# Decode step: sample index and state outputs moved among the state tiles, value projection and gated unit into the top-k, sample state onto GpSimd

## The reference

```python
u, q, k, v, qi, ki, wi = split(rmsnorm(x) @ w_in)        # q, k: per-head norm and rotary; qi, ki: rotary
# state-space heads: 32 groups, 64 complex states each
bu = einsum('blgc,gpc->blgp', u, b_bar)
a_cum, h = associative_scan(combine, (lam_bar, bu)); h = h + a_cum * h0
y = real(einsum('blgp,gcp->blgc', h, c_mat)) + d_skip * u
y = gelu(y); y = y * sigmoid(y @ w_glu)
# sparse attention: 8 heads of 64
s = sum_h wi[h] * relu(qi[h] . ki)                       # the samples also score 256 cached keys each
idx = top_k(s, 64); attend over the chosen k, v
x = x + concat(y, attention) @ w_out
```

## Time and profile before

| | |
|---|---|
| median of 3 runs | 1687.07 us (1686.31 to 1692.87) |
| the profiled execution | 1684.85 us, its span 1683.0 us |
| TensorE, VectorE, ScalarE, GpSimd busy | 93%, 76%, 57%, 5% of the span |
| mean granted TensorE clock | 0.956 |
| loads at the start | params 1152 and 142 KB, x 1120 KB, consts 861 KB, weights of u 2048 KB |
| other transfers at the start | old pool history 448 KB, weights of qi 2048 KB, of kw 288 KB |

### The profile page before, as it was taken

The page is one execution under the profiler, slowest core; times in us unless marked ns, Lnnn a source line. Parts: engine busy times, 40 slices in busy tenths (PEclk is TensorE's granted clock), DMA queues, the critical chain, the costliest instruction groups (busy, mean ns, idle before and its releaser), DMA issues.

```text
span 1683.0 us, 23394 instructions
## 1 busy us (share of the span) xinstructions
PE 1571.4 (93%) x7789; PEld 1268.0 (75%) x7789; DVE 1274.4 (76%) x1704; ACT 963.7 (57%) x1222; POOL 87.2 (5%) x118
## 2 busy tenths in 40 slices
PE   5997949889999778999999999999999999999998
PEld 4653436479999666888888888888888888888887
DVE  8888561135554467988988998998998998988986
ACT  2110324134443226777777777777777777777774
POOL 0386100000000000000000000000000000000000
PEclk9998778999999977999999999999999999999999
DMA  5421012424535515998998998998998998998992
GB/s 217 150 76 50 30 54 72 140 100 161 190 120 172 203 35 187 356 378 305 353 374 310 347 373 312 348 370 312 355 358 324 349 363 320 348 362 325 348 358 94
DMA packets 212886, 420.79 MB, mean 250 GB/s; under 512 B 10233, under 2 KB 56469, under 8 KB 212572
## 3 DMA queue, kind: packets, MB, share of 16 engines
q1 hardware_dynamic: 211542, 414.37, 68.6%
q10 hardware_dynamic: 622, 3.45, 0.5%
q0 software_dynamic: 672, 2.32, 0.4%
HBM read 417.50 MB, written 3.07 MB: 250 GB/s over the span
## 4 chain that ended last, share of the span: by engine, by line
PE 83%; DVE 3%; issue 2%; ACT 1%; DMA 1%; SPq 0%; DVEq 0%; ACTq 0%
PE bank L1149 19%; PE bank L1154 19%; PE bank L1153 19%; PE bank L1027 3%; PE bank L1030 3%; PE bank L1031 3%; PE bank L1104 3%; PE bank L1010 2%; PE bank L1174 1%; PE bank L1112 1%; PE bank L1042 1%; PE bank L1046 1%; PE bank L1045 1%; PE bank L744 1%; DVE hT L1561 1%
## 5 line engine op out<-in xcount | busy, mean ns | idle before, releaser
L2047 DVE TENSOR_TENSOR split<-raw_w,split 128x1024 fp32r<-128x1024 f32 x672 | 783.3, 1220 | 50.6 <-ACT split L1498 48.5
L1498 ACT ACTIVATE split<-raw_w 128x1024 fp32r<-128x1024 f32 x672 | 684.4, 1060 | 109.3 <-PE bank L1149 108.1
L1149 PE MATMUL bank<-split,xgr 128*128 128x512 f32 x896 | 359.2, 401 | 3.7 <-DVE split L2047 3.7
L1154 PE MATMUL bank<-split,xgr 128*128 128x512 f32 x896 | 354.4, 396 | 0.0
L1153 PE MATMUL bank<-split,xgr 128*128 128x512 f32 x896 | 354.4, 396 | 0.0
L1149 PEld LDWEIGHTS bank<-split,xgr 128*128 128x128 f32 x896 | 169.3, 189 | 41.9 <-DVE split L2047 4.5
L1154 PEld LDWEIGHTS bank<-split,xgr 128*128 128x128 f32 x896 | 169.2, 189 | 39.9
L1153 PEld LDWEIGHTS bank<-split,xgr 128*128 128x128 f32 x896 | 169.4, 189 | 37.5
L1149 PE MATMUL bank<-split,hbr 128*128 128x512 f32 x448 | 177.9, 397 | 0.0
L1154 PE MATMUL bank<-split,hbr 128*128 128x512 f32 x448 | 176.9, 395 | 0.0
L1153 PE MATMUL bank<-split,hbr 128*128 128x512 f32 x448 | 176.9, 395 | 0.0
(11 more groups left out here) (377 smaller groups left out, 1913.6 us busy)
## 6 DMA issues: line engine op xcount, KB each, us to landing
raw_w<-in_moe_gate SPq DMA_DIRECT2D x112, 1024.0 KB, 5.4
raw_w<-in_moe_up SPq DMA_DIRECT2D x112, 1024.0 KB, 6.0
raw_w<-in_moe_down SPq DMA_DIRECT2D x112, 1024.0 KB, 5.2
ring<-in_w_gate SPq DMA_DIRECT2D x11, 1024.0 KB, 5.0
ring<-in_w_up SPq DMA_DIRECT2D x11, 1024.0 KB, 7.3
ring<-in_w_down SPq DMA_DIRECT2D x8, 1408.0 KB, 6.2
ring<-in_w_in SPq DMA_DIRECT2D x5, 2048.0 KB, 9.7
ring<-in_w_out SPq DMA_DIRECT2D x2, 2048.0 KB, 7.6
```

The source lines that it names most:

```text
L1149: first = mm(out, hi, place[:, s, 0, cols], start=start, stop=False)
L1154: last = mm(out, hi, place[:, s, 1, cols], start=False, stop=stop)
L1498: A(place[:, s, 0, :], raw_w[:, at:at + BLOCK], ACT.Copy).then_inc(sem("high_ready"), 1)
L2047: TT(place[:, s, 1, :], raw_w[:, at:at + BLOCK], place[:, s, 0, :].bitcast(F32), ALU.subtract).then_inc(sem("low_ready"), 1)
```

## The change

- **Order of fills.** The value projection leaves the state tiles; its three fills go before `glu`, behind it, and between the logits of t = 0 and t = 1. The sample index (`skT`, `wbd`) and the state outputs y 0 to 2 go among the state tiles, y 3 between the index dots of t = 0 and t = 1, `kt` behind the logits of t = 2.
- **State outputs.** The samples' y no longer needs the finished sample state: it is summed from `raw` through the same matrices as the prompt and from `hs0` = rates times h0, so two more 8-column matmuls per tile.
- **GpSimd** computes `hs0` before tile 0, the sample state and the last state behind tile 15, and fills `qbd`.
- **VectorE** does the factors and `norm` ahead of all doublings (`NORM_AT` = 1), the index queries behind the rotary of qi, the skip terms where y stands, the gelu argument before the top-k and the gelu behind its first round (`GELU_AT` = 1).
- **SyncE** loads the first weights after x and consts, the sample pages earlier, and `wout1` behind the first two samples' pages.
- Buffers: `ga`, `gb`, `kisT`, `srelu` move, the gated output stays in `uT`.

```diff
-NORM_AT = 32
+NORM_AT = 1
+GELU_AT = 1
...
+def index_order():
+    dots = [("dot", t, h) for t in range(TC) for h in range(H)]
+    return dots[:H] + [("y", 3)] + dots[H:]
...
-    groups = [[], four("qis") + ["kis", "wiT"], [("q", 0)], [("q", 1)], [("q", 2)], [("q", 3), "qn"],
-              [("k", 0)], [("k", 1)], [("k", 2)], [("k", 3), "kn"], four("qs"), [("v", 0)], four("qe"),
-              [("v", 1)] + four("ks"), [("v", 2)], four("ke")]
+    groups = [[], four("qis") + ["kis", "wiT"], [("q", 0)], [("q", 1), "wbd"], [("q", 2)], [("q", 3), "qn"],
+              [("k", 0)], [("k", 1)], [("k", 2)], [("k", 3), "kn"], four("qs") + keys(0, 1), keys(2, 3, 4),
+              four("qe") + keys(5), keys(6, 7) + four("ks"), ["kidT", ("y", 0), ("y", 1)], four("ke") + [("y", 2)]]
...
-    f += ["kidT", "wbd"]
-    f += [("skT", b) for b in range(NB)]
-    f += [("dot", t, h) for t in range(TC) for h in range(H)]
-    f += [("kt", t) for t in range(TC)]
-    f += [("y", c) for c in range(4)] + [("glu", c) for c in range(4)]
+    f += index_order()
+    f += [("v", 0)] + [("glu", c) for c in range(4)] + [("v", 1)]
...
-    f += logits(0) + logits(1) + probs_T(0) + [("att", 0)] + logits(2) + [("attT", 0)] + probs_T(1) + [("att", 1)]
+    f += logits(0) + [("v", 2)] + logits(1) + probs_T(0) + [("att", 0)] + logits(2)
+    f += [("kt", t) for t in range(TC)] + [("attT", 0)] + probs_T(1) + [("att", 1)]
...
+            def state_outputs(jc):
+
+                if jc == 0:
+                    pe.wait_ge(sem("out_mats"), 1)
+                    pe.wait_ge(sem("carried"), 1)
+                out = open_fill(("y", jc))
+                pe.wait_ge(sem("raw_taken"), 2 * (4 * jc + 4))
+                pe.wait_ge(sem("states"), 4 * jc + 4)
+                for q in range(4):
+                    j, rows = 4 * jc + q, slice(32 * q, 32 * q + 32)
+                    mm(out[rows, 0:NP_], cf4[:, j, 0, :], er3[:, j, :], start=True, stop=False)
+                    mm(out[rows, 0:NP_], cf4[:, j, 1, :], ei3[:, j, :], start=False, stop=True)
+                    mm(out[rows, NP_:T], cf4[:, j, 0, :], raw[:, j, 0, :], start=True, stop=False)
+                    mm(out[rows, NP_:T], cf4[:, j, 1, :], raw[:, j, 1, :], start=False, stop=False)
+                    mm(out[rows, NP_:T], c_m[:, j, 0, :], hs0[:, j, 0, :], start=False, stop=False)
+                    last = mm(out[rows, NP_:T], csn3[:, j, :], hs0[:, j, 1, :], start=False, stop=True)
+                last.then_inc(full(("y", jc)), 1)
...
+            emptied(dve, ("y", 3))
+            dve.wait_ge(sem("last_state"), 1)
+            yv = uT.rearrange("p c t -> p (c t)")
+            link(TT(ga, yv, yv, ALU.mult))
+            link(TS(ga, ga, 0.044715, 1.0, ALU.mult, ALU.add))
+            TT(ga, ga, yv, ALU.mult).then_inc(sem("gelu_arg"), 1)
+
             m8 = mx8.rearrange("p (t k) -> p t k", t=TC)
             for r in range(TOPK // 8):
+                if r == GELU_AT:
+                    dve.wait_ge(sem("gelu_tanh"), 1)
+                    link(STT(gb, gb, 1.0, yv, ALU.add, ALU.mult))
+                    TS(yv, gb, 0.5, None, ALU.mult).then_inc(sem("gelu"), 1)
+                    dve.wait_ge(sem("gelu"), 1)
...
-            exps(0, 0, H)
+            exps(0, 0, 4)
+            copy_rows(("v", 2), z3["v"])
+            exps(0, 4, H)
             exps(1, 0, 4)
             copy_probs(0, 0)
             copy_probs(0, 1)
             exps(1, 4, H)
-            copy_T(("attT", 0), ycat[:, 4:8, :], 0, QN[0])
+            for t in range(TC):
+                copy_rows(("kt", t), z3["k"])
+            copy_T(("attT", 0), h3[:, 4:8, :], 0, QN[0])
```

More of the change, by code:

```diff
@@ L208 @@
 PT_FILLS = [2, 4, 1]
[L209 removed]
+PROMPT_FILLS = ("logit", "pT", "att", "attT", "kt")
+LOOP_END = ("dot", 0, 0)
 FILLS = fill_order()
@@ L415, in hybrid_step @@
         pT = [tk(1024), tk(2048), tk(384)]
+        assert at[0] >= m1 + 2 * NJ * NP_ and H * KN[0] + 8 * T <= 2 * NJ * NP_
+        ga, gb = [ring[:, m1 + H * KN[0] + k * 4 * T:m1 + H * KN[0] + (k + 1) * 4 * T] for k in range(2)]
         kb = tk(2 * 1024).rearrange("p (r g d) -> p r g d", r=2, g=2)
@@ L803, in channels, with index_dots, index_keys @@
                 last.then_inc(full(name), 1)
+            sdot = ps("sdot")
+            def index_dots(b):
+                emptied(pe, ("skT", b))
+                last = mm(sdot[0:64, 0:PAST], qib3[0:HD, b, :], kisT[0:HD, b % 2, :], start=(b == 0), stop=(b == NB - 1))
+                last.then_inc(full("sdot") if b == NB - 1 else sem("sample_dots"), 1)
+            def index_keys(b):
+                if b == 0:
+                    pe.wait_ge(sem("sample_index_q"), 1)
+                    pe.wait_ge(sem("ki_ready"), 1)
+                    for s in range(NB):
+                        mm(sdot[0:64, PAST:SK], qib3[0:HD, s, :], kiT[0:HD, NP_ + s:NP_ + s + 1], start=(s == 0), stop=(s == NB - 1))
+                    pe.wait_ge(sem("kidx_in"), 16 * 2 * NB)
+                out = open_fill(("skT", b))
+                for g in range(2):
+                    last = nc.tensor.transpose(out[0:HD, g * P:(g + 1) * P], kin[:, b, g, :], ident)
+                last.then_inc(full(("skT", b)), 1)
+                if b:
+                    index_dots(b - 1)
@@ L872, in _ @@
-            pe.wait_ge(sem("kidx_in"), 16 * 2 * NB)
-            for b in range(NB):
-                out = open_fill(("skT", b))
-                for g in range(2):
-                    last = nc.tensor.transpose(out[0:HD, g * P:(g + 1) * P], kin[:, b, g, :], ident)
-                last.then_inc(full(("skT", b)), 1)
-                if b:
-                    index_dots(b - 1)
-            index_dots(NB - 1)
-            for t in range(TC):
-                for h in range(H):
-                    half = slice(HD * (h % 2), HD * (h % 2) + HD)
-                    out = open_fill(("dot", t, h))
-                    mm(out[0:QN[t], 0:KN[t]], qiT3[half, h // 2, t * P:t * P + QN[t]], kiT[half, 0:KN[t]],
-                       start=True, stop=True).then_inc(full(("dot", t, h)), 1)
@@ L889, in _ @@
-            emptied(pe, "sdot")
-            emptied(pe, "wbd")
-            mm(ps("sscore")[32:40, 0:SK], wbd[0:64, 0:NB], srelu[0:64, :], start=True, stop=True).then_inc(full("sscore"), 1)
-            emptied(pe, ("ke", 3))
-            for t in range(TC):
-                out = open_fill(("kt", t))
-                for c in range(4):
-                    last = nc.tensor.transpose(out[0:TCN[t], c * P:(c + 1) * P], kT3[:, c, t * P:t * P + TCN[t]], ident)
-                last.then_inc(full(("kt", t)), 1)
@@ L924, in _ @@
                 nq = QN[t]
-                if kind == "logit":
+                if name == ("logit", 1, 0):
+                    value_rows(2)
+                if kind == "kt":
+                    out = open_fill(name)
+                    for c in range(4):
+                        last = nc.tensor.transpose(out[0:TCN[t], c * P:(c + 1) * P], kT3[:, c, t * P:t * P + TCN[t]], ident)
+                    last.then_inc(full(name), 1)
+                elif kind == "logit":
                     h = name[2]
@@ L1738, in _ @@
-            dve.wait_ge(sem("sample_state"), 1)
-            dve.wait_ge(sem("zeroed"), 1)
-            for hh in range(2):
-                half = slice(HD * hh, HD * hh + HD)
-                for c in range(4):
-                    at = 2 * c + hh
-                    last = nc.vector.tensor_copy(qibd[0:HD, at:at + 72 * (NB - 1) + 1:72], qiT3[half, c, NP_:T])
-            last.then_inc(sem("sample_index_q"), 1)
-            filled(dve, "wbd")
-            TT(wbd[0:64, 0:NB], ps("wbd")[0:64, 0:NB], const("bsel")[0:64, :], ALU.mult).then_inc(free("wbd"), 1)
```

300 lines of the change are left out of this document (161 added, 139 removed).

## The result

The changed kernel took 1667.95 us (median of 4 runs, 1664.53 to 1673.98) beside 1689.7 us for the kernel before on the same chips (1686.31 to 1692.87). The ratio is 0.9875, 95% interval 0.9838 to 0.9913. The profiled execution took 1667.89 us, 17.0 less than that of before (1684.85); the medians moved by 21.75. Forecast were 1664 for the median and -23.4 between the profiled executions.

A forecast was written before the change was run, and what follows sets the result against it. VectorE and TensorE nearly fill the state tiles; the change targets the sample-state and top-k stretches, which no engine fills. Terms -3.2 + 4.7 - 15.1 - 17.1 + 7.3 = -23.4 us gave a median of 1664, range 1652 to 1680.

The forecast's parts named there:

- c: From tile 15's end to the end of the dots: sample state and transposes leave the chain, -15.1 us, bounds -12 to -18.
- d: From the dots' end to the first mask: VectorE's wait of 11.04 and other work go, hidden by TensorE, -17.1 us.
- a: Start: the norm stands behind the factors, not the small doublings, so the first tile moves by -3.2 us.
- b: State tiles: value projections leave, y, skip terms and index-query copies come, +4.7 us, bounds 0 to +13.
- The contention rival: During the dots: GpSimd's sample state slows VectorE's sums by a tenth, +1 us, inside the range; no chance of its own.
- e: Attention: v of t = 2 between the logits counts 7.05 us, `kt` 0.3; +7.3 us, bounds +4 to +10.
- f: The rest of the kernel: 0 us, since loads of the last weights are issued well before their use.
- The low clock: Rival: state outputs y and matmuls of tiles 14 and 15 run at the low clock, +15 us, 1679; chance 0.18.
- The high clock throughout: Rival: TensorE never rests long from tile 12 to attention; -6 us or so, 1658; chance 0.15.
- the loss below the kernel before: Rival: the low clock lasts through the top-k as well, +11 us, 1698, slower than before; chance 0.04.

The follow-up runs named there:

- experiment 3: Changed kernel with y 3 moved behind all index dots; 1663.39 us, ratio 0.9842 to the kernel before.
- experiment 5: Changed kernel with y 3 behind all dots, and v of t = 2 and the transposes of k behind v of t = 0; 1656.74 us, ratio 0.9813.
- experiment 8: Changed kernel with y 0 to 2 taken out of the state tiles and set ahead of y 3; 1671.89 us, ratio 0.99.
- the first experiment: Changed kernel with v of t = 2 moved from between the logits to right behind v of t = 0; 1665.34 us, ratio 0.9843.
- experiment 10: Changed kernel with the sample index spread over the groups of tiles 2 to 9; 1674.97 us, ratio 0.9921.

## Why the prediction came out as it did

The forecast of -23.4 is near the 21.75 by which the medians moved. Between the profiled executions 6.4 us of it are missing: 4.2 in the attention, 2.8 behind it and 0.7 ahead of the sums, less 1.0 more at the start and small differences. The nearness is in part luck: the tiles, right to 0.2 here, took 4 us more in another execution of the same code.

No run put the sample index, the value projection as a whole or gelu back where they stood. So c and d rest on the traces: the waits of 15.35 (VectorE's, before the first sum) and 11.04 are gone, the stages have the lengths of the remaining terms, and experiments 3, 5 and 8 move their ends. The wait of 15.35 in the kernel before:

```profile
187.66 0.35 DVE L1756 SCALAR_TENSOR_TENSOR ring<-ring,low,consts 128x128 f32<-128x128 f32 x1 [15.35 <-ACT ring L1327]
```

**a. Start.** Forecast -3.2, measured -4.2, and u starts where it was put only with the old loads (21.70 against the forecast 21.6). The order of loads was entered at nothing, with up to -5 as a bound: it brought the params 2.1 us earlier (VectorE's first instruction at 2.92 against 4.99), 2.15 at u, and all but 0.6 was given back in u at the lower clock. In other executions of the same start less was given back, and the first tile began up to 1.3 earlier. So the term was mis-sized by 1.0 to 2.3, by a part named among its bounds.

**b. State tiles.** The sum was right (+4.7 against +4.5), its composition wasn't. The wait ahead of tile 14 was 1.2 (and 0.36 for ScalarE's copy), not 4.5, for y 0 and y 1 ran wholly at clock 1.00 in this execution. At that clock a fill took 4.28 (y 0 from 143.94 to 148.22), not 3.8; the two more matmuls per tile had no term. In the first experiment's execution of the same code they began at 0.50 and VectorE waited 1.73 and 3.68. The eight index-query copies cost 1.8 us together, where 0.9 was put in, and the skip terms 1.5. VectorE is busy 2.9 us longer (93.10 against 90.16) and idle 1.5 longer, where the sum had 2.3 and 2.4. Without y in the tiles they took 3.8 us less (experiment 8).

**c. To the end of the sums.** 21.9 against 21.2. GpSimd's last tile ended 4.9 after VectorE's, y 3 took 6.1. The dots of t = 0 were slower beside GpSimd (seven in 4.79 where before 2.83), hidden by the wait for y 3. The contention rival named this with a tenth; it was 69%, and it cost nothing.

**d. To the first mask.** 27.25 against 27.3. Slack of TensorE 1.95, forecast 0.5 to 2.

**e. Attention: the step that failed, in its size.** Measured +11.5, beyond the bounds of +4 to +10 as well. The mechanism was named (v of t = 2 on a full engine, the exps behind its copy). ScalarE shows it, waiting for v of t = 2 with exps in line behind:

```profile
221.03 0.59 ACT L1329 ACTIVATE low<-bank 24x512 f32<-24x512 f32 x1 [5.03 <-PE bank L839]
```

The price of v was 7.05; taking it away returned 5.7 alone and 6.6 with `kt` gone as well. The term that was too small is that of `kt`: put at 0.3 because TensorE had idle time, it returned 2.9 alone and 3.8 with v gone. Both together return 9.5. Two stretches of the changed kernel show where the time passes: five us in which TensorE waits for ScalarE, which is busy with exps and copies, then five at the lower clock.

```profile
224.00:229.00 5.00, 2.46 (x14) 2.49 (x14) 0.97 (x7) 4.36 (x16) 0.00 (x0) 0.80 0.85 325
229.00:234.00 5.00, 5.00 (x24) 2.20 (x24) 3.58 (x17) 0.00 (x0) 0.00 (x0) 0.52 0.00 0
```

About 2 of the 11.5 stay without a cause shown by a run: with both blocks gone the attention took 30.8 against 28.8 before.

**f. The rest.** Of 0 forecast, 1.9 came in the sample logits: TensorE waits 1.56 and 1.74 us for cached keys where it waited 1.17 before. No run took this apart. Such waits are in all changed runs, from 0.65 together (experiment 8) to 3.3 (the changed kernel), and wout1's load, which stands behind the first pages in all of them, wasn't moved alone. The last 0.9 have no cause shown.

**The rivals.** The low clock did come, though not where it was put: it stood ahead of y, from 117 to 142, and y itself ran at 1.00 in most profiled executions. Stretches of the changed kernel, and of the first experiment's:

```profile
122.00:142.00 20.00, 18.95 (x42) 9.26 (x41) 15.18 (x32) 2.22 (x8) 14.48 (x21) 0.51 0.00 1
142.00:152.00 10.00, 10.00 (x96) 5.71 (x97) 9.32 (x13) 1.11 (x5) 1.69 (x4) 1.00 0.00 0
```

```profile
127.00:147.00 20.00, 20.00 (x53) 9.66 (x52) 15.02 (x28) 2.60 (x10) 12.13 (x17) 0.50 0.00 1
```

The same code thus took 4 us more in the tiles (106.3 and 110.4) with the clock returning later. The four times of the changed kernel spread over 9.5; how much of that is this, unprofiled executions can't tell. The rival's price for tiles 14 and 15 was too high: 5.6 each was TensorE's whole work per tile, while a tile's own matmuls took 1.2 at 1.00 and 2.2 at 0.50. The rule of the Trainium skill that the prediction set beside this rival ("TensorE: Matmul & The Clock Gate", Part 4, PE-mode transpose) bears on the busy stretch from 122 to 142, with 18.95 of 20 us busy at 0.51. But the sample index's transposes are only 2.5 of those 18.95 us (four times 0.63), and the trace of experiment 10 has the same clock from 127 to 142 without them, with TensorE busy 8.68 of 15. What sets it in the changed kernel stays open. The high clock throughout and the loss below the kernel before did not happen.

## What to carry over

When a block is moved under another engine's work, look at both ends: what is left at its old place, and whether there is a gap in the new cover that holds another block for nothing; here a 4.8 us wait took 7 us of matmuls without cost, as the next block then ran at clock 1.00. Price a block put into a full engine's stretch by what waits behind it on the other engines too: 8.6 us of matmuls cost at least 9.5. Put work that waits for another engine behind all work that doesn't: y 3 behind all dots was worth 4.7 us.

## What the hardware showed

- A sooner start can be given back by the clock: u began 2.15 us earlier, at clock 0.50 for its first five us, and took 18.30 in place of 15.42. In ten other executions with the same start it took 16.73 to 18.19.
- The same 32 matmuls of `glu` took 10.71 us behind a wait of 4.80, and 7.81 at clock 1.00 with no wait ahead.
- Identical tile code had the clock back at 1.00 at 142 us in one execution and at about 149 in another, and took 106.3 and 110.4.
- VectorE instructions can take longer while GpSimd works: some of those on 128x32 took 0.40 us (others 0.18) and 0.18 to 0.19 without GpSimd, and the seven weighted sums of the dots of t = 0 took 4.79 in place of 2.83.
